# Latent attention started with four of eight heads, recurrence gates moved into a dense unit, and convolution taps and rank sums moved

## The reference

```
def hybrid_mixer(h, positions, w_in, b_in, ...):
    proj = h @ w_in + b_in
    pa, pb, pc, pg = ...                       # recurrence, attention, convolution, gates
    xa = causal_depthwise_conv(pa[..., :512], lru_conv_w, lru_conv_b)       # 4 taps
    y_a = (rg_lru(xa, lru_w_gate, lru_b_gate, lru_lambda) * gelu(pa[..., 512:])) @ lru_w_out
    y_b = mla_branch(cq, ckv, kpe, ...)        # ranks 384 and 256, 8 heads of 64 + 32
    y_c = conformer_conv_branch(pc, ...)       # causal convolution, 31 taps, layer norm
    merged = sigmoid(g0) * y_a + sigmoid(g1) * y_b + sigmoid(g2) * y_c
    return merged @ w_out
```

## Time and profile before

| | |
|---|---|
| median of 3 runs | 3688.31 us (3684.47 to 3688.48) |
| profiled execution, its own time | 3684.93 us |
| its span, first to last instruction | 3683.1 us |
| mean granted TensorE clock | 0.980 |
| PE busy | 3511.1 us, 95% of the span |
| DVE busy | 2468.7 us, 67% |
| ACT busy | 1629.7 us, 44% |

### The profile page before, as it was taken

How to read it: one execution, slowest core, us unless ns; L and a number is a source line. 1 busy time by engine, 2 the same in 40 slices (tenths; PEclk the granted TensorE clock), 3 DMA queues, 4 the chain that set the end, 5 groups by cost and what they waited for, 6 DMA issues and landing times.

```text
span 3683.1 us, 49529 instructions
## 1 busy us (share of the span) xinstructions
PE 3511.1 (95%) x19557; PEld 2932.4 (80%) x19557; DVE 2468.7 (67%) x3520; ACT 1629.7 (44%) x2417; POOL 55.2 (2%) x82
## 2 busy tenths in 40 slices
PE   7989999989999999999899999999999989999999
PEld 5668987757998799876477889889988656778997
DVE  7558854647882788466765598549864777558862
ACT  4535543444562366235423355425542543244552
POOL 0000000000000000000000000000000000000000
PEclk9999999989999999999899999999999999999999
DMA  4212323202332233332123223323333212222332
GB/s 133 69 46 92 104 92 105 86 29 75 104 115 92 69 105 115 94 95 55 35 69 91 92 92 105 105 89 104 104 98 102 66 46 58 80 92 92 104 105 84
DMA packets 340156, 321.06 MB, mean 87 GB/s; under 512 B 31769, under 2 KB 312165, under 8 KB 339941
## 3 DMA queue, kind: packets, MB, share of 16 engines
q1 hardware_dynamic: 335588, 307.95, 26.9%
q0 software_dynamic: 2560, 8.26, 0.7%
q10 hardware_dynamic: 1792, 1.88, 0.2%
HBM read 315.94 MB, written 2.10 MB: 86 GB/s over the span
## 4 chain that ended last, share of the span: by engine, by line
PE 79%; DVE 14%; ACT 4%; issue 2%; ACTq 0%; POOL 0%; DVEq 0%; POOLq 0%
PE products L757 29%; PE products L896 23%; PE products L794 6%; PE small L794 6%; PE small L896 4%; PE products L1097 2%; DVE conv L2672 2%; DVE w_lo L1965 1%; DVE seven_x L2198 1%; ACT w_hi L1384 1%; PE products L1271 1%; PE small L955 1%; DVE X L1980 1%; DVE x_sums L2187 1%; PE products L1119 1%
## 5 line engine op out<-in xcount | busy, mean ns | idle before, releaser
L1965 DVE TENSOR_TENSOR w_lo<-raw,w_hi 128x2048 fp32r<-128x2048 f32 x190 | 435.2, 2291 | 501.7 <-ACT w_hi L1384 501.0
L1384 ACT ACTIVATE w_hi<-raw 128x2048 fp32r<-128x2048 f32 x190 | 363.3, 1912 | 893.3 <-PE products L757 641.5
L757 PE MATMUL products<-a_hi,w_hi 128*128 128x512 f32 (+1 forms) x1216 | 500.8, 412 | 35.6 <-DVE a_lo L2020 12.0
L757 PE MATMUL products<-a_lo,w_hi 128*128 128x512 f32 (+1 forms) x1216 | 488.4, 402 | 0.0
L757 PE MATMUL products<-a_hi,w_lo 128*128 128x512 f32 (+1 forms) x1216 | 487.8, 401 | 0.0
L896 PE MATMUL products<-seven_x,w_hi 128*128 128x256 f32 x2592 | 467.7, 280 | 8.5 <-DVE w_lo L2227 4.1
L896 PEld LDWEIGHTS products<-seven_x,w_hi 128*128 128x128 f32 x2592 | 397.8, 189 | 12.0 <-DVE w_lo L2227 5.4
L896 PE MATMUL products<-seven_x,more_hi 128*128 128x256 f32 x1632 | 381.4, 283 | 2.3 <-ACT rs_b L1474 2.3
L896 PE MATMUL products<-seven_x,w_lo 128*128 128x256 f32 x1296 | 364.1, 281 | 0.0
L757 PEld LDWEIGHTS products<-a_hi,w_hi 128*128 128x128 f32 (+1 forms) x1216 | 233.3, 192 | 102.8 <-issue 43.6
L896 PEld LDWEIGHTS products<-seven_x,more_hi 128*128 128x128 f32 x1632 | 282.2, 191 | 3.1 <-ACT rs_b L1474 3.1
(11 more groups left out here) (434 smaller groups left out, 7427.3 us busy)
## 6 DMA issues: line engine op xcount, KB each, us to landing
raw<-in_ffn_w SPq DMA_DIRECT2D x244, 512.0 KB, 4.3
raw<-in_w_in SPq DMA_DIRECT2D x108, 512.0 KB, 4.8
raw<-in_w_ffn_in SPq DMA_DIRECT2D x88, 512.0 KB, 4.4
raw<-in_w_ffn_out SPq DMA_DIRECT2D x40, 512.0 KB, 4.6
raw<-in_w_out SPq DMA_DIRECT2D x32, 512.0 KB, 4.3
raw<-in_ffn_w SPq DMA_DIRECT2D x24, 384.0 KB, 3.6
raw<-in_w_mem_kv SPq DMA_DIRECT2D x8, 512.0 KB, 4.1
dft<-in_dft POOLq DMA_DIRECT2D x2, 2048.0 KB, 9.5
```

The lines of the kernel that those rows point to most:

```text
L757: mm = pe.matmul(G[pair][0:m, into + b, 0:n], w[:, s, at:at + m], x, start=(first or into > 0) and k == 0 and q == 0, stop=(last or ends) ...
L1384: act.activation(w_hi[:, s, :], raw[:, s, :], ACT.Copy).then_inc(hi_ready, 1)
L1965: dve.tensor_tensor(w_lo[:, s, :], raw[:, s, :], w_hi[:, s, :].bitcast(F32), ALU.subtract).then_inc(lo_ready, 1)
```

## The change

- **Gates.** Gates 0 and 1 stand as before; gates 2 and 3 are now hooks inside the next dense unit, after 12 and after 21 of its 48 matmuls.
- **Rank sums.** In the dense unit the sums stand after 12 matmuls, not 6, and the spread after 33, not 27.
- **Taps.** Before the rank roots 1 tap instead of 8; after them 5 instead of 2, and 4 new ones between the scaling of the ranks and the low parts of their operands; 18 instead of 24 in attention; then 8 instead of 12 in each gate unit, and 4 after each of the six branch pieces of the first three rounds.
- **Heads.** The first query piece of heads 4 to 7 doesn't wait for the bank of the piece two before. The turned part of those queries goes to the free half of a `G` bank, not to `B5`. PE starts attention when heads 0 to 3 are turned, and waits for the rest before the scores of head 2. DVE turns heads 4 to 7 behind the scores of head 0.
- **Space.** The probability tiles lie in slot 1 of `w_lo`, slot 1 of `w_hi`, and in the place of two tables. So chunks 5 to 7 of `a_hi` and `a_lo` stay, and `leave` makes chunks 0 to 4 alone (`LEFT_CHUNKS`). Only slot 0 can hold a ready unit in attention: its low part is made behind head 1, and the second unit is split after attention.
- **End of attention.** The first gate unit starts in `G[1]` (`other_group`) without a wait for the last output of attention, which the second gate unit has instead.

```diff
-CONV_SHARE = 12
+CONV_SHARE = 8
+LEFT_CHUNKS = ((0, 1), (2, 3), (4,), ())
...
-    mla_prob = [place(f"mla_prob{i}", [P, ROWS_4], at=BROADCASTS + 4 * ROWS_4 * i) for i in range(2)]
+    mla_prob = [place(f"mla_prob{i}", [P, ROWS_4], at=at)
+                for i, at in enumerate((W_LO + 4 * UNIT, W_HI + 4 * UNIT, BROADCASTS))]
...
-    mla_prob.append(place("mla_prob2", [P, ROWS_4], at=REGION_A + 26 * KB))
...
+                    if i in heads_ready:
+                        heads_ready[i]()
...
+            def other_group():
+
+                if c.group % 2 == 0:
+                    c.group += 1
...
-                for i in range(LC):
+
+                def recurrence_gates(i):
...
+                recurrence_gates(0)
+                recurrence_gates(1)
+                take_unit()
+                piece(full_two_parts, hooks={(0, 4): lambda: recurrence_gates(2), (0, 7): lambda: recurrence_gates(3)})
                 c.one("sig_ready", 4)
-                take_unit()
-                piece(full_two_parts)
...
-                piece(full_two_parts, hooks={(0, 2): rank_sums, (1, 1): lambda: spread_groups(totals, (B4[:], B5[:]))})
+                piece(full_two_parts, hooks={(0, 4): rank_sums, (1, 3): lambda: spread_groups(totals, (B4[:], B5[:]))})
...
-                    pe.matmul((B4, B5)[u][:], rot_pe[:], X[:, u, :], start=True, stop=True).then_inc(rot_ready, 1)
+                    pe.matmul((B4[:], G[beside][:, 1, :])[u], rot_pe[:], X[:, u, :], start=True, stop=True).then_inc(rot_ready, 1)
...
+                def first_heads():
+
+                    pe.wait_ge(rot_used, c.next("rot_used", 2))
+                    pe.wait_ge(rope_ready, c.next("rope_ready", MLA_HEADS))
+
+                def other_heads():
+
+                    pe.wait_ge(even_read, c.next("even_read"))
+                    all_read_out()
+                    pe.wait_ge(rot_used, c.next("rot_used"))
+                    pe.wait_ge(rope_ready, c.next("rope_ready", MLA_HEADS))
+
+                latent_attention({0: first_heads, 2: other_heads})
+                other_group()
...
+                        if (j, b) == (0, 1):
+                            pe.wait_ge(o_used, c.now("o_used"))
...
-                        conv_taps(8)
+                        conv_taps(1)
                 group_roots(RANKS, rank_squares)
-                conv_taps(2)
+                conv_taps(5)
...
+                conv_taps(4)
                 dve.wait_ge(src_ready, c.now("src_ready"))
...
+                turned_keys(range(4))
+                queries_out(0)
+                turned_queries(0, B4[:])
+                turned_keys(range(4, MLA_HEADS))
+                beside_turned = queries_out(1)
...
+                def beside(h):
+
+                    if h == 1:
+                        split_lo()
+                    elif h:
+                        conv_taps(3)
+
+                latent_attention(leave, beside, other_heads)
+                split_lo()
+                other_group()
...
-                        conv_taps(CONV_SHARE if 2 * j + b < 5 else len(todo))
+                        conv_taps(CONV_SHARE if 2 * j + b < 6 else len(todo))
...
+                        if j < DC // 2 - 1:
+                            conv_taps(CONV_SHARE // 2)
```

More of the change, by code:

```diff
@@ L264, in two_blocks @@
     raw = place("raw", [P, 2, UNIT])
+    W_HI = top[0]
     w_hi = place("w_hi", [P, 2, UNIT], F32R)
@@ L1311, in _ @@
                         pe.wait_ge(even_read, c.next("even_read"))
-                    heads_piece([[(head_columns(k, QK, slice(0, 4), slice(HEAD, QK)), both(k)) for k in range(3)]])
+                    turned_in = c.group % 2
+                    heads_piece([[(head_columns(k, QK, slice(0, 4), slice(HEAD, QK)), both(k)) for k in range(3)]],
+                                copied=u == 1)
                     pe.wait_ge(even_read, c.next("even_read"))
@@ L1315, in _ @@
                                  for b in range(2)])
[L1316 to L1324, removed]
-                pe.wait_ge(al_ready, c.next("al_ready", DC))
+                    rotated(u, turned_in)
+                def first_heads():
[8 more added lines that the diff above has]
+                other_group()
+                pe.wait_ge(al_ready, c.next("al_ready", len(sum(LEFT_CHUNKS, ()))))
                 pe.wait_ge(branch_ready, c.next("branch_ready", LC))
@@ L2383, in ffn, with latent_attention @@
                 low_and_square((DC - 2, DC - 1), next_gain)
-            def latent_attention(leave, beside):
+            def latent_attention(leave, beside, other_heads):
                 for i in range(MLA_HEADS + 3):
@@ L2810, in _, with turned_keys, turned_queries @@
                 settled()
-                for h in range(MLA_HEADS):
-                    dve.tensor_copy(kv_head[turn, h, :], craw[turn, 5, :]).then_inc(rope_ready, c.one("rope_ready"))
-                for u in range(2):
-                    piece()
-                    p = group()
-                    dve.wait_ge(pe_copied, c.next("pe_copied"))
-                    taken(dve.memset(tiny[:, 1, :], 0.0), p)
-                    odd_heads(q_head, 4 * u)
-                    split_lo()
+                split_lo(6)
+                def turned_keys(heads):
+                    for h in heads:
+                        dve.tensor_copy(kv_head[turn, h, :], craw[turn, 5, :]).then_inc(rope_ready, c.one("rope_ready"))
+                def turned_queries(u, product):
                     dve.wait_ge(rot_ready, c.next("rot_ready"))
-                    dve.tensor_tensor(X[:, 2 + u, :], (B4, B5)[u][:], sinT[:], ALU.mult).then_inc(rot_used, c.one("rot_used"))
+                    dve.tensor_tensor(X[:, 2 + u, :], product, sinT[:], ALU.mult).then_inc(rot_used, c.one("rot_used"))
                     stepped(dve.tensor_tensor(X[:, u, :], X[:, u, :], cosT[:], ALU.mult))
@@ L2828, in _, with queries_out, other_heads @@
                                           ALU.add).then_inc(rope_ready, c.one("rope_ready"))
-                dve.wait_ge(rope_ready, c.now("rope_ready"))
+                def queries_out(u):
+                    piece()
+                    p = group()
+                    dve.wait_ge(pe_copied, c.next("pe_copied"))
+                    taken(dve.memset(tiny[:, 1, :], 0.0), p)
+                    odd_heads(q_head, 4 * u)
+                    return p
+                turned_keys(range(4))
[3 more added lines that the diff above has]
+                beside_turned = queries_out(1)
+                def other_heads():
+                    turned_queries(1, G[beside_turned][:, 1, :])
+                    dve.wait_ge(rope_ready, c.now("rope_ready"))
                 pair = iter(range(LC))
```

33 lines of the change are left out of this document (21 added, 12 removed).

## The result

The changed kernel takes 3619.12 us (median of 4 runs, 3619.05 to 3619.36), the kernel before 3686.39 us beside it. The ratio is 0.9818, with a 95% interval from 0.9801 to 0.9835: 1.8% faster. The forecast was 3623, from 3607 to 3642. The profiled execution has a span of 3617.3 us against 3683.1, so 65.8 us went.

What follows compares the result with a forecast made beforehand. PE, busy 95% of the span, was taken as the bound, so only its waits and slow stretches give time. Terms of 33.3 and 29.2 us, together 62.5, from 3684.9 gave 3622.4, stated as 3623; range 3607 to 3642.

Steps and rivals of the forecast that it cites:

- C: Start of attention: two waits go, a 3.7 us one appears; gain 12.0 us first layer, 10.0 second; bounds 7 to 14.5.
- A: Recurrence gates: no wait before gate 2, 4.0 us less per layer; bounds 0 to 4.0.
- B: Rank sums: 4.4 us less per layer, wait before heads' units growing to about 3 or 4; bounds 3 to 7.
- D: Chunks kept in attention: fewer ACT and DVE instructions in `leave`, 0.5 us gained ahead of the last head per layer.
- E: End of attention: the 2.79 us wait and its slow clock go, 4.6 us first layer, 4.3 second; bounds 2.8 to 4.6.
- F: Gate rounds: waits behind branch pieces go, with slow clock 7.8 us first layer, 6.0 second; bounds 2 to 7.9.
- rival 2: The thin cover of F fails and its four waits stay at part or whole: 3630 to 3638 us, chance 0.13.
- Rival 1: Low clock stays through attention's first heads, costing 4.9 us more a layer: 3633 us, chance 0.16.
- Rival 3: More gained: new waits in B and C leave the clock up, other slow stretches go: 3617 or 3610; beyond 3613, 0.12.
- Rivals 4 and 5: 4: DVE bounds every attention head, 3650, chance 0.02; 5: later waits absorb gains, within 7 us of before, 0.03 including oversights.

## Why the prediction was right

The direction, the size and nearly every wait came out as written. The measured gain was 67.3 us between medians, the sum was 62.5. By the table, 2.9 of the 4.2 us between the two mixer layers and the sum lie in C, and 1.4 in A and B.

- **A** held: no wait before gates 2 and 3, and undoing it costs 7.1 us.
- **B**'s ends held in sum (8.8 and 9.4 for A and B, 8.4 expected), and the wait left ahead of the heads' units was 2.92 and 3.91, "about 3 or 4". One step was too simple: "four taps, 2.6 us, on the path" counted all of the taps, but 2.1 us passed behind the unit's end without them too, and taking the taps away gave 0.8 and 1.8. The term also priced the taps and the sums' place as one. The runs with one half undone show that either half gives most of it, and that they overlap; no run undid both.
- **C** was undersized: 13.7 and 11.2 us against 12.0 and 10.0. Its instants were right: 0.77 and 3.69 us where 0.8 and 3.7 came out of the working, both named after DVE. What was mis-sized is the slow clock, 2.5 us taken off a layer. Set against the 14.5 and 12.5 without it, the layers lost 0.8 and 1.3. Behind the wait of 3.69 it was 8.4 and 8.2 us from head 2's scores to head 3's, where later heads follow each other by 6.8: 1.7 and 1.4 of slow clock, not 2.0. The 0.5 for B's longer wait was not lost in the first layer, whose first scores came 28.0 us behind the start of the heads' units where the working has 28.4; in the second it was 28.7. How C's gain divides is in part shown: without the early start 11.3 us of the 24.9 go, with the low part ahead 7.2; the bank that the second query unit no longer waits for was not undone.
- **D and E** held to 0.1 us in both layers, and the window at 1.00 shows the clock's part.
- **F** held: no wait, the taps done before the mean, and 112.1 us twice. The cover, worked out as 0.2 to 0.3 us, is 0.37, so rival 2 did not come about, though one tap more would have begun it.
- **Rival 1**, the half clock through the first heads, did not happen here, but it is real: it came when a wait of 4.74 us stood ahead of all scores, and in part when three waits of 1.5 to 2.5 us followed each other. The Trainium skill, "TensorE: Matmul & The Clock Gate", section "A second HAM failure mode: psum-queue depth-cycling", says that short idling between groups of matmuls can make the clock swing. The run with the low part ahead agrees: head 0's scores ran at 1.00, head 1's, behind a wait of 2.33, at 0.50. For waits of 0.36 to 1.24 us the traces disagree: in attention's steady part and with the sums behind head 0 the clock stayed at 1.00.
- **Rival 3** did not come about: the new waits did not leave the clock up, in B (0.63 and 0.50 behind them) or in C (0.58). The slow work merely cost less there than was taken off. Rivals 4 and 5 had nothing for them: in attention's steady part one head follows the other by 6.77 us, in the kernel before and after.

## What to carry to other kernels

Follow a stalled stage instant by instant through all engines, including the wait that comes next; the sum of stretches was right to 6% here, while most errors were in edits looked at alone. At the start of this attention it was cheaper to let PE wait behind two heads' scores at full clock, and in pieces of about a microsecond, than once ahead of the stage; that this holds elsewhere is not shown. Two edits at one bottleneck overlap, so undo each alone before saying which one gained.

## What the runs showed of the hardware that was not expected

Waits of 0.77, 0.86 and 1.24 us left the granted clock at 1.00. Waits of 2.0 to 2.8 us were mostly followed by slow work, which cost some 1.8 us in the gate rounds, but waits of equal length ended both ways. The 4 us behind one of 2.46 ran at 0.59 in one layer and 1.00 in the other, and behind one of 2.12 ahead of the heads' units at 0.60 with the taps off the path, at 1.00 with the sums or the taps at their old place. What decides between the two is not shown. The wait of 4.74 us ahead of short bursts was followed by 14 us at 0.50 in the first layer; in the second head 2's scores, 10.2 us later, ran at 1.00. After 3.69 us the clock was 0.58 in one stretch of 4.1 us.

The stage that no edit touches varies more than some edits give. The first gate starts at 1651.02, 1654.14, 1656.38 and 1658.56 us in four kernels whose programs are equal up to there. Their windows show where: granted clock of one stretch of the first model, in the kernel with the sums behind head 0 and in that with the taps off the path.

```profile
800.00:1000.00 200.00, 188.66 (x1162) 166.31 (x1161) 151.88 (x202) 95.03 (x142) 4.20 (x6) 0.98 0.25 80
```

```profile
800.00:1000.00 200.00, 187.40 (x1113) 162.92 (x1114) 149.81 (x204) 93.18 (x138) 4.22 (x6) 0.96 0.23 75
```

Added up over windows of 25 us to 1650 us, the share of the clock that was not granted comes to 35.8, 37.8, 39.5 and 43.0 us in the four, in the order of their starts. So the clock falls for longer in one execution than in another, among many short waits, and an estimate from these sums gives 7.2 of the 7.5 us between the first and the last start. Why it falls at other instants each time stays open.
